# Where the small DMAs of a hybrid attention stage are issued, and what TensorE waits for behind it

## The reference

```python
def hybrid_mixer(h, w_in, b_gate, q_norm, k_norm, rel_bias, w_branch_a, w_branch_b, w_out, cos, sin):
    proj = h @ w_in                                  # 1024 -> 8192
    pa, pq, pk, pv, pg = ...                         # a: q, k, v of 24 heads; b: q, k, v; gates 2 x 1024
    for g, (window, dil) in enumerate(DILATED_GROUPS):
        o, lse = dilated_group_attention(..., bias_groups[:, g], dil, window // (2 * dil))
    wgt = jax.nn.softmax(jnp.stack(lses, axis=0), axis=0)
    o_a = jnp.sum(wgt[..., None] * jnp.stack(outs, axis=0), axis=0)
    o_b = gqa_axial_attention(q_b, k_b, v_b, q_norm, k_norm, cos, sin)
    gates = jax.nn.sigmoid((pg + b_gate).reshape(B, S, N_BRANCHES, D))
    merged = gates[:, :, 0] * (o_a @ w_branch_a) + gates[:, :, 1] * (o_b @ w_branch_b)
    return merged @ w_out
```

## Time and profile before

| | |
|---|---|
| median of three executions | 3387.72 us (3386.49 to 3396.03) |
| profiled execution | 3396.03 us; span 3394.0 us; mean granted TensorE clock 0.924 |
| PE busy | 2968.2 us, 87% of the span |
| PE weight load | 2595.1 us, 76% |
| DVE busy | 1982.3 us, 58% |
| ACT busy | 1434.8 us, 42% |
| chain that ended last | PE 70%, DVE 14%, ACT 6% |
| DMA queues | q1: 456.51 MB; q10: 13.06 MB; mean 139 GB/s |

### The profile page before, as it was taken

How to read it: one execution, slowest core, us unless ns; L and a number is a source line. 1 busy time by engine, 2 the same in 40 slices (tenths; PEclk the granted TensorE clock), 3 DMA queues, 4 the chain that set the end, 5 groups by cost and what they waited for, 6 DMA issues and landing times.

```text
span 3394.0 us, 43922 instructions
## 1 busy us (share of the span) xinstructions
PE 2968.2 (87%) x17510; PEld 2595.1 (76%) x17510; DVE 1982.3 (58%) x2349; ACT 1434.8 (42%) x1781; POOL 0.9 (0%) x9
## 2 busy tenths in 40 slices
PE   6987898989489899675887799998799899989898
PEld 5876787879378778674776588787688787988887
DVE  4665666663656556655555566666566665655565
ACT  4444445443344444332212344445444544444444
POOL 0000000000000000000000000000000000000000
PEclk9997899999689999786998799999799999999899
DMA  7643565644056565330000365654355664753563
GB/s 222 189 131 91 165 190 164 192 136 156 1 155 187 164 184 169 111 112 1 1 1 21 117 187 171 183 176 125 100 176 172 182 185 115 212 160 100 174 187 93
DMA packets 639646, 471.49 MB, mean 139 GB/s; under 512 B 56001, under 2 KB 607297, under 8 KB 639508
## 3 DMA queue, kind: packets, MB, share of 16 engines
q1 hardware_dynamic: 616968, 456.51, 44.6%
q10 hardware_dynamic: 22540, 13.06, 1.5%
HBM read 466.63 MB, written 1.84 MB: 138 GB/s over the span
## 4 chain that ended last, share of the span: by engine, by line
PE 70%; DVE 14%; ACT 6%; PEld 4%; issue 2%; ACTq 1%; PEldq 1%; DVEq 1%; DMA 1%; SPq 0%
PE pair_bank L337 23%; PE pair_bank L338 12%; PE pair_bank L481 11%; PE out_banks L350 5%; PE out_banks L352 5%; PE out_banks L351 5%; PEld out_banks L481 3%; DVE low L273 2%; ACT high L269 2%; PEldq L229 1%; DVE mix L1898 1%; PE pair_bank L1739 1%; DVEq L229 1%; PE out_banks L683 1%; PE pair_bank L1752 1%
## 5 line engine op out<-in xcount | busy, mean ns | idle before, releaser
L273 DVE TENSOR_TENSOR low<-raw,high 128x3072 fp32r<-128x3072 f32 (+3 forms) x328 | 948.1, 2891 | 863.4 <-ACT high L269 863.4
L337 PE MATMUL pair_bank<-x_parts,high 128*128 128x512 f32 x3520 | 1252.0, 397 | 34.0 <-DVE low L273 28.9
L338 PE MATMUL pair_bank<-x_parts,low 128*128 128x256 f32 x3520 | 992.1, 282 | 0.0
L269 ACT ACTIVATE high<-raw 128x3072 fp32r<-128x3072 f32 (+3 forms) x328 | 784.8, 2393 | 376.5 <-PE out_banks L352 200.3
L337 PEld LDWEIGHTS pair_bank<-x_parts,high 128*128 128x128 f32 x3520 | 667.7, 190 | 193.1 <-DVE low L273 27.8
L338 PEld LDWEIGHTS pair_bank<-x_parts,low 128*128 128x128 f32 x3520 | 673.2, 191 | 9.4
L377 ACT ACTIVATE sq_scratch<-pair_bank 128x512 f32<-128x512 f32 x220 | 131.5, 598 | 584.9 <-PE pair_bank L338 584.9
L350 PE MATMUL out_banks<-high,hid_h 128*128 128x512 f32 x880 | 349.5, 397 | 12.3 <-DVE hid_l L411 12.3
L351 PE MATMUL out_banks<-low,hid_h 128*128 128x512 f32 x880 | 348.6, 396 | 0.0
L352 PE MATMUL out_banks<-high,hid_l 128*128 128x512 f32 x880 | 348.5, 396 | 0.0
L481 PE MATMUL pair_bank<-x_parts,high 128*128 128x256 f32 x1216 | 235.6, 296 | 39.4 <-DVEq L229 31.0
(11 more groups left out here) (348 smaller groups left out, 3100.0 us busy)
## 6 DMA issues: line engine op xcount, KB each, us to landing
raw<-in_ffn_w_in_dram SPq DMA_DIRECT2D x352, 512.0 KB
raw<-in_ffn_w_out_dram SPq DMA_DIRECT2D x176, 512.0 KB
raw<-in_ffn_w_dram SPq DMA_DIRECT2D x132, 512.0 KB
raw<-in_w_in_dram SPq DMA_DIRECT2D x32, 1024.0 KB
raw<-in_gla_w_in_dram SPq DMA_DIRECT2D x12, 1024.0 KB
raw<-in_rwkv_w_rkv_dram SPq DMA_DIRECT2D x12, 1024.0 KB
raw<-in_swa_w_qkv_dram SPq DMA_DIRECT2D x10, 1024.0 KB
raw<-in_swa_w_o_dram SPq DMA_DIRECT2D x8, 1024.0 KB
```

Source lines behind the costliest of these rows:

```text
L269: nc.scalar.activation(high[u % SPLIT][:, lo:w], raw[u % RAW][:, lo:w], ACT.Copy).then_inc(high_ready, count)
L273: nc.vector.tensor_tensor(low[u % SPLIT][:, lo:w], raw[u % RAW][:, lo:w], high[u % SPLIT][:, lo:w].bitcast(F32), ALU.subtract).then_inc(we ...
L337: nc.tensor.matmul(o, H[:, w], x_parts[:, k, :], start=(k == 0), stop=False)
L338: last = nc.tensor.matmul(o[:, 0:SEQ], L[:, w], xh[:, k, :], start=False, stop=(k == KB - 1))
```

## The change

The 62 DMAs move from SP's stream to ACT's; `beside_sp` goes, and SP issues only weight loads. The two stores follow the table copies at c = 0, behind a wait of ACT on its own copies, and the eight gate biases follow them at once (before: one in each of c = 10 to 17). The far biases are loaded at c = 4 (before: c = 8), near 0 and 1 at c = 20, the v_far copies at c = 21 and 23, and near x + 2 in `exps(x)`, behind its wait for a_max. Both sigmoid parts stand at c = 31, the second behind a wait for the last evacuation. `branch_a_wait` goes: PE enters branch a through the barrier.

```diff
-                if st.beside_sp is not None:
-                    st.beside_sp(env, sp, st, c)
...
-        elif c == 8:
-            sp.wait_ge(e.named("table_stored"), 32)
...
-        elif GATE_AT + 4 <= c:
-            at = 2 * (c - GATE_AT - 4)
-            for x in (at, at + 1):
-                if 2 <= x + 1 < A_JOBS:
-                    sp.wait_ge(e.named("a_max"), x)
-                    load_near(e, sp, x + 1)
...
         def exps(x):
             act.wait_ge(e.named("a_max"), x + 1)
+            if x + 2 < A_JOBS:
+                load_near(e, act, x + 2)
...
+            e.link_act(act, s_.activation(rows[:, NEAR:NEAR + FAR], e.turn_bank[1][0:A_HEADS, 0:FAR], ACT.Copy))
+            act.dma_start(io["t_near"], ...).then_inc(e.named("table_stored"), 16)
+            act.dma_start(io["t_far"], ...).then_inc(e.named("table_stored"), 16)
+            for n in range(2 * D // CH):
+                act.dma_start(gate_bias(e, n), ...).then_inc(e.named("gate_bias_loaded"), 16)
+        elif c == 4:
+            act.wait_ge(e.named("table_stored"), 32)
...
+        elif c == V_AT + 2:
+            load_near(e, act, 0)
+            load_near(e, act, 1)
+        elif c in (V_AT + 3, GATE_AT - 1):
+            g = 1 if c == V_AT + 3 else 2
+            act.wait_ge(e.emptied, st.e0 + c + 1)
...
-            act.wait_ge(e.emptied, st.e0 + GATE_AT + 4)
-            sigmoids(e, 0)
+            for branch in range(2):
+                act.wait_ge(e.emptied, st.e0 + (GATE_AT + 4 if branch == 0 else END))
+                for t in range(NT):
+                    last = s_.activation(gates(e, t, branch), gates(e, t, branch), ACT.Sigmoid)
+                last.then_inc(e.named("gates_ready"), 1)
...
-    def branch_a_wait(e, pe, k):
-        if k == 0:
-            pe.wait_ge(e.emptied, stages[3].e0)
-        pe.wait_ge(e.named("a_low"), 2 * k + 2)
...
-            sigmoids(e, 1)
...
-            dve.wait_ge(e.named("gates_ready"), 1)
+            dve.wait_ge(e.named("gates_ready"), 2)
```

More of the change, by code:

```diff
@@ L2318, in load_near @@
                 src = bass.AP(tb.tensor, at + b * (NEAR - 1), [[NEAR - CLASSES * STEP, STEP], [NEAR - CLASSES, STEP], [1, SEQ]])
[L2319 to L2333, removed]
-        elif c == 8:
-            sp.wait_ge(e.named("table_stored"), 32)
[L2336 to L2356, removed]
-                                 v_staged(e, t, g, slice(n, P, CLASSES))).then_inc(e.named("v_placed"), 16)
-        elif GATE_AT + 4 <= c:
-            at = 2 * (c - GATE_AT - 4)
-            for x in (at, at + 1):
-                if 2 <= x + 1 < A_JOBS:
-                    sp.wait_ge(e.named("a_max"), x)
-                    load_near(e, sp, x + 1)
@@ L2365, in beside_act @@
+                act.dma_start(near[x % 2](e.mix)[b * CLASS:(b + 1) * CLASS, o, :], src).then_inc(e.named(f"near{x % 2}_loaded"), 16)
     def beside_act(e, act, st, c):
@@ L2393, in beside_act @@
             s_.activation(rows[:, 0:NEAR], e.turn_bank[0][0:A_HEADS, :], ACT.Copy)
-            s_.activation(rows[:, NEAR:NEAR + FAR], e.turn_bank[1][0:A_HEADS, 0:FAR], ACT.Copy).then_inc(e.named("table_copied"), 1)
+            e.link_act(act, s_.activation(rows[:, NEAR:NEAR + FAR], e.turn_bank[1][0:A_HEADS, 0:FAR], ACT.Copy))
+            act.dma_start(io["t_near"], rows[0:A_PER, 0:NEAR].unsqueeze(1).to_broadcast([A_PER, NEAR_COPIES, NEAR])).then_inc(
+                e.named("table_stored"), 16)
+            act.dma_start(io["t_far"], rows[A_PER:A_HEADS, NEAR:NEAR + FAR].unsqueeze(1)
+                          .to_broadcast([A_HEADS - A_PER, FAR_COPIES, FAR])).then_inc(e.named("table_stored"), 16)
+            for n in range(2 * D // CH):
+                act.dma_start(gate_bias(e, n), spread(io["b_gate_2"][0][n * CH:(n + 1) * CH])).then_inc(e.named("gate_bias_loaded"), 16)
+        elif c == 4:
+            act.wait_ge(e.named("table_stored"), 32)
+            tb = io["t_far"]
+            for b in range(2):
+                for n in range(2):
+                    src = bass.AP(tb.tensor, tb.offset + (b ^ n) * A_PER * FAR_COPIES * FAR + CLASS - 1,
+                                  [[FAR - 1, CLASS], [FAR_COPIES * FAR, A_PER], [1, CLASS]])
+                    act.dma_start(far_bias(e, slice(b * CLASS, (b + 1) * CLASS))[:, :, n * CLASS:(n + 1) * CLASS], src).then_inc(
+                        e.named("far_loaded"), 16)
         elif c == Q_AT + 2:
@@ L2644, in hybrid @@
               Stage("proj", chunks=chunks, dest="gate", evac=evac, by="act", beside_pe=beside_pe, beside_act=beside_act,
[L2645 removed]
+                    beside_dve=beside_dve),
               back("w_branch_a_2", dest="gate", evac=evac_a, by="dve", beside_pe=branch_a_pe, beside_act=branch_a_act,
[L2647 removed]
+                   beside_dve=branch_a_dve, x=lambda e: (tails(e.high, 4), tails(e.low, 4))),
               back("w_branch_b_2", dest="gate", evac=evac_b, by="dve", beside_pe=branch_b_pe, beside_act=branch_b_act,
```

15 lines of the change are left out of this document (8 added, 7 removed).

## The result

The changed kernel took 3422.3 us in the median of four executions (3420.08 to 3426.07), beside 3387.1 us (3384.54 to 3396.03) for the kernel before on the same chip. The ratio is 1.0100, with a 95% interval of 1.0080 to 1.0121. The prediction was 3422, with a range of 3405 to 3434. The profiled execution took 3428.41 us, its span 3426.6, at a mean granted clock of 0.919.

What follows compares the result with a forecast made beforehand. PE paces the first 24 units, an ACT-DVE chain the last eight; ACT has 0.9 us slack. Terms 2.9 + 5.9 + 6.6 + 14.7 + 3.8 = 33.9, say 34, on the 3387.72 median: 3422 us, range 3405 to 3434.

Steps and rivals of the forecast that it cites:

- Rival 1: Every burst after an emptying: issues fit into ACT's idle 3.4 us per unit; -5 us, 3383; chance 0.06.
- Term A: Unit 0: stores and gate biases delay rounding, PE +6.4 us; the 3.49 stall at unit 4 goes; net +2.9.
- Rival 2: ACT's queue fills behind t_far's 1024 rows, so later bursts, near loads included, wait; +46 us, 3434; chance 0.10.
- the upper bound: Queue fills behind stores (+4), far biases at 6.3 (+2), two more clock falls in gate chunks (+5): +45 us, 3433.
- Term B: Far biases after unit 4: 4.3 us of issues less 0.9 slack plus 2.5 clock, +5.9.
- Term C: Near and v_far bursts at c = 20 and 21: first stalls PE and slows its clock, second hidden; +6.6 us.
- Term D: c = 23 and gate chunks: second v_far burst, near loads ahead of exponentials and an uncovered table load; +14.7 us.
- Term E: Border to branch a: PE stands at the barrier until all four sigmoids end; 2.4 plus 1.4 slow clock, +3.8 us.

Runs made afterwards that it cites:

- the doses of two and six: Kernel before, with two gate-bias loads issued by ACT at c = 10 and six at c = 13; 3393.08 us in one execution.
- Issues by GpSimd: Kernel before, with the two stores and all 32 near loads issued by the idle POOL under the same waits; 3385.05 us, ratio 0.9985.
- Biases in single file: Changed kernel, with the eight gate-bias loads taken out of c = 0 and issued by ACT one by one at c = 10 to 17; 3415.12 us.
- v_far copies alone: Kernel before, with only the sixteen v_far copies moved to ACT, at c = 21 and 23; 3403.11 us, ratio 1.0039.
- near loads alone: Kernel before, with only the 32 near loads moved to ACT, at c = 20 and in the first six exps; 3408.3 us, ratio 1.0053.
- The reordering: Changed kernel, with each job's four near loads issued behind the two exponentials instead of ahead; 3422.28 us in one execution.
- the mended versions: Kernel before, with stores and near loads on POOL (3385.05 us), or on SP with stores one step later and near loads one step earlier (3384.05 us).

## Why the prediction was right, and where it was not

**The mechanism held.** An issue holds ACT's stream, ACT's idle time is not slack, and the sum lies on the path. Rival 1 (not slower) is refuted in its strong form by each L269 with "<-issue" and by the doses of two and six: by the slack of 0.9 and the 0.6 beside the emptying, PE notices what goes beyond 1.3 to 1.5 us (an estimate; two issues of 0.86 left no gap, four of 2.71 left 1.39). In its weak form it holds: an issue does run beside an ACTIVATE that has begun, and the order that uses it gained 5.8 us besides the table load. The rule of the Trainium skill that I set beside it (DMA: Bandwidth & Descriptors, Issuing engines are not separate DMA queues), that issue time is usually small beside the DMA itself, agrees with the bias loads ahead of the stores: an issue took 0.45 us, and the load landed 2.7 to 3.5 us after its start. What fails is what I had drawn from it, that the move would be worth next to nothing: 62 issues moved and the kernel lost 35 us.

**Term A was too small by 6.** It said 6.9 for the burst and 6.4 for PE; the trace has 14.2 and 13.4. The step that failed is "gate biases seven times 0.56 and once 1.08": I took prices from SP, where no store stood ahead. Behind the two stores the first three took 4.34, 3.08 and 2.53. Rival 2 had this mechanism at +4; its argument against itself ("there a weight load of 1024 rows was the next one, here loads of 128 rows") was wrong, since the bias load of 128 rows took 4.34 all the same. That SP's 4.35 was due to the stores, as rival 2 and the upper bound took it, is not shown: with the stores on POOL, SP's weight loads in the same place took as long (SP's timeline, "Issues by GpSimd"):

```profile
2868.35 3.55 SPq L298 DMA_DIRECT2D raw<-in_w_in_dram  x1
2873.62 4.65 SPq L298 DMA_DIRECT2D raw<-in_w_in_dram  x1
```

On ACT the stores are shown to be the cause, by the same loads ahead of them. Rival 2's other half, near loads that grow too, did not come.

**Term B was too large by 4.3.** It had 4.3 for the four issues, 0.9 of slack, and 2.5 for the clock. They took 2.71, began beside the emptying, and left PE a wait of 1.39 with no fall of the clock; the fall in the earlier trace rows stood behind 3.49. The step that failed is the price, taken from a crowded SP queue, and that I let none of it run beside the emptying: that made a wait of 3.4, and with it the fall of the clock that I charged to waits of over 3 us. That limit does not hold either: the clock fell behind 1.83 in "Biases in single file" and not behind 3.62 in "v_far copies alone".

A and B miss in opposite directions and leave 1.8 us of the sum (35.75 against 33.9). The time of 3422 is in part luck; with A alone mis-sized it would have been 3428.

**Term C** was right (6.35 for 6.6), and for its reason: near loads alone and v_far copies alone cost 5.5 more in sum than together, and PE's wait of 4.77 behind the v_far burst is there only when that burst comes alone.

**Term D** had the right size (14.9 for 14.7), but part of its reason fell. I charged the issues ahead of the exponentials to ACT's time as such. The reordering shows that of these 14.9 some 7 are due to their place: behind the exponentials they run partly beside work that ACT already has, what DVE and PE wait for comes sooner, and the table load (1.28, which I had priced) is covered again. The drain that the Trainium skill adds to a table load (ScalarE: Activation LUTs, What ACT_TABLE_LOAD costs) is missing here too; ACT's timeline at the border, after:

```profile
3136.89 1.28 ACT L2406 ACT_TABLE_LOAD   x1
3138.18 3.89 ACT L2406 ACTIVATE raw<-raw 128x1024 f32<-128x1024 f32 x4
```

**Term E** was right at the border itself (3.84 for 3.8), but 1.5 of it is gone some units on, where the clock fell in the kernel before and not in the change. Done alone it costs 4.5, then 3.0, in the trace, and the time does not confirm it.

**What stays open.** Which property of a store holds the queue (the broadcast from few partitions, the 1024 rows, or the write to HBM) was not tried apart, nor what lengthens SP's weight loads. Nor is it settled why the clock falls in one execution and not in another.

## What to carry to other kernels

Before moving DMA issues to an engine that looks idle, compute the slack behind its idle time, not the idle time: here ACT idled 3.4 us per unit and 0.9 of it was free. Put issues behind the work that others wait for, put small loads ahead of a store on the same queue, and do not send a row of them behind one: here the same eight loads cost 12.4 us behind the stores and 3.7 ahead of them. Where one queue's wait blocks a weight load, try first to move it by a step: here one number mended it without burdening another engine. And where a transfer lands late, look at what was issued ahead of it on any queue before you change its issuer.

## What the runs showed of the hardware

- On ACT, bias loads are held behind two stores in their own queue: 4.34, 3.08 and 2.53 us for the first three issues. Ahead of the stores they took 0.33 to 0.45, alone 0.34. Weight loads on SP took 3.55 and 4.65 with no store in their queue, so the 4.35 of the earlier trace rows need not be due to stores.
- Near loads that POOL issued just after SP's weights landed 6.3 to 9.6 us after their start, against a median of 3.4 for all 32: a separate issuer does not keep them apart from the weights.
- A DMA issue on ACT starts 0.01 us after the start of an ACTIVATE and runs beside it. It costs ACT only what reaches beyond.
- The clock does not fall every time. Over the 5.76 us behind the wait of 3.5 to 3.6 us at unit 4, PEclk was 0.50 in the kernel before and 1.00 in that with v_far copies alone; behind 4.15, with near loads alone, it was 0.70; behind 1.83, in "Biases in single file", 0.70 too. The time of the first matmul alone does not tell: it was 0.39 in both kernels at 1.00 and at 0.70, and 0.58 in that at 0.50. Over 10 us around one wait of 2.7 us PEclk was 0.66, 0.83 and 1.00 in three kernels. This moves a stage by 1.5 to 3 us from one profiled execution to the next, and may be why the mended versions gain 8.3 us in their trace and about 5 in the median; that was not tested.
